# High and low parts of the normed x laid out 64 bytes further in SBUF, in a two-block transformer on one core

## The reference, cut to what matters

```python
# block 1, each of 2 layers
xn = _rms_norm(x, attn_norm[l]);  h = xn @ w_in[l]          # 3 kinds of attention follow
x = x + mix @ w_o[l]
xn = _rms_norm(x, ffn_norm[l])
gate, up = jnp.split(xn @ w_gate_up[l], 2, axis=-1)
x = x + (jax.nn.silu(gate) * up) @ w_down[l]
# block 2, each of 2 layers
h = rmsnorm(x, norm_mix_pre[l]);  u = h @ w_in[l]           # pool, conv and dilated attention, gates
x = x + rmsnorm(merged @ w_out[l], norm_mix_post[l])
h = rmsnorm(x, norm_mem_pre[l])                             # attention to a memory of 256 tokens
h = rmsnorm(x, norm_ffn_pre[l]);  u = h @ w_up[l]
x = x + rmsnorm(y, norm_ffn_post[l])                        # y = (silu(conv(ua)) * ub) @ w_down
```

## Time and profile before

| | |
|---|---|
| median of three runs | 1726.08 us |
| the profiled execution's own time | 1727.64 us |
| its span, first to last instruction | 1725.8 us |
| TensorE matmul busy (PE) | 1690.0 us, 98%, 13590 instructions |
| stationary loads busy (PEld) | 1629.3 us, 94% |
| VectorE busy (DVE) | 1196.2 us, 69% |
| ScalarE busy (ACT) | 895.0 us, 52% |
| GpSimd busy (POOL) | 113.4 us, 7% |
| DMA | 274.31 MB, mean 159 GB/s |
| granted TensorE clock, mean | 0.995 of 2.4 GHz |

### The profile page before, as it was taken

One profiled execution on the slowest core, in us unless ns is written; L12 is line 12 of the kernel. 1 busy time (PEld: TensorE's weight loads), 2 busy tenths in 40 slices (PEclk: granted clock), 3 DMA queues, 4 the chain that ended last, 5 costly groups with the idle time before them and its releaser, 6 DMA issues.

```text
span 1725.8 us, 31850 instructions
## 1 busy us (share of the span) xinstructions
PE 1690.0 (98%) x13590; PEld 1629.3 (94%) x13590; DVE 1196.2 (69%) x1745; ACT 895.0 (52%) x1366; POOL 113.4 (7%) x72
## 2 busy tenths in 40 slices
PE   9989999999999999999999999999999999999997
PEld 9978999999789999989999989999899999899997
DVE  5886766557966675476858768873667767669863
ACT  5575544454765444544445755544434446656542
POOL 2020000020100000210000110001100001010000
PEclk9999999999999999999999999999999999999999
DMA  7313555553235555645335335554444345345551
GB/s 287 104 58 126 186 188 177 169 199 122 82 95 199 187 179 189 219 161 184 111 128 189 130 129 202 187 171 174 156 156 164 133 158 187 117 147 187 198 179 42
DMA packets 52830, 274.31 MB, mean 159 GB/s; under 512 B 6096, under 2 KB 6736, under 8 KB 52560
## 3 DMA queue, kind: packets, MB, share of 16 engines
q1 hardware_dynamic: 52544, 271.22, 46.2%
q10 hardware_dynamic: 144, 1.05, 0.2%
HBM read 271.19 MB, written 1.05 MB: 158 GB/s over the span
## 4 chain that ended last, share of the span: by engine, by line
PE 81%; DVE 12%; ACT 3%; issue 2%; DMA 1%; SPq 0%; ACTq 0%; DVEq 0%
PE bank L775 17%; PE bank L778 17%; PE bank L777 17%; PE scores L775 3%; PE scores L777 3%; PE scores L778 3%; DVE weights_lo L647 3%; PE heads L775 2%; PE heads L777 2%; PE heads L778 2%; DVE x_lo L900 1%; PE scores L1849 1%; ACT probs L1170 1%; PE heads L1877 1%; DVE x L2340 1%
## 5 line engine op out<-in xcount | busy, mean ns | idle before, releaser
L647 DVE TENSOR_TENSOR weights_lo<-raw,weights_hi 128x1536 fp32r<-128x1536 f32 (+2 forms) x344 | 584.2, 1715 | 252.4 <-ACT weights_hi L636 252.0
L636 ACT ACTIVATE weights_hi<-raw 128x1536 fp32r<-128x1536 f32 (+4 forms) x352 | 499.6, 1439 | 222.6 <-PE bank L778 88.8
L775 PE MATMUL bank<-x_hi,weights_lo 128*128 128x256 f32 (+1 forms) x1600 | 458.8, 287 | 0.9 <-DVE weights_lo L647 0.9
L778 PE MATMUL bank<-x_hi,weights_hi 128*128 128x256 f32 (+1 forms) x1600 | 452.4, 283 | 0.0
L777 PE MATMUL bank<-x_lo,weights_hi 128*128 128x256 f32 (+1 forms) x1600 | 452.4, 283 | 0.0
L775 PEld LDWEIGHTS bank<-x_hi,weights_lo 128*128 128x128 f32 (+1 forms) x1600 | 304.8, 190 | 6.2 <-issue 4.8
L777 PEld LDWEIGHTS bank<-x_lo,weights_hi 128*128 128x128 f32 (+1 forms) x1600 | 304.8, 191 | 2.0 <-issue 2.0
L778 PEld LDWEIGHTS bank<-x_hi,weights_hi 128*128 128x128 f32 (+1 forms) x1600 | 304.9, 191 | 0.0
L775 PE MATMUL bank<-hidden_hi,weights_lo 128*128 128x256 f32 x704 | 194.6, 276 | 0.0
L777 PE MATMUL bank<-hidden_lo,weights_hi 128*128 128x256 f32 x704 | 194.3, 276 | 0.0
L778 PE MATMUL bank<-hidden_hi,weights_hi 128*128 128x256 f32 x704 | 194.3, 276 | 0.0
(11 more groups left out here) (410 smaller groups left out, 3414.0 us busy)
## 6 DMA issues: line engine op xcount, KB each, us to landing
raw<-in_w_b SPq DMA_DIRECT2D x194, 768.0 KB, 4.2
raw<-in_w_a SPq DMA_DIRECT2D x120, 768.0 KB, 4.3
raw<-in_w_a SPq DMA_DIRECT2D x16, 512.0 KB, 4.1
raw<-in_w_b SPq DMA_DIRECT2D x10, 512.0 KB, 4.3
raw<-in_w_b SPq DMA_DIRECT2D x2, 752.0 KB, 4.7
raw<-in_w_a SPq DMA_DIRECT2D x2, 736.0 KB, 8.1
raw<-in_w_b SPq DMA_DIRECT2D x2, 720.0 KB, 4.7
raw<-in_w_a SPq DMA_DIRECT2D x2, 672.0 KB, 7.4
```

The costliest lines, as they stand in the source:

```text
L636: nc.scalar.activation(whi[c % SPLIT][:, 0:n], raw[c % RAW][:, 0:n], ACT.Copy).then_inc(*s.mark("weights_hi", c))
L647: nc.vector.tensor_tensor(wlo[c % SPLIT][:, 0:n], raw[c % RAW][:, 0:n], whi[c % SPLIT][:, 0:n].bitcast(F32), ALU.subtract).then_inc(*s.mar ...
L775: ins = nc.tensor.matmul(dst, wl, xh, start=start, stop=False, skip_group_check=skip)
L778: ins = nc.tensor.matmul(dst, wh, xh, start=False, stop=stop, skip_group_check=skip)
```

## The change

The 64-byte tile minus_half is placed ahead of x_hi and no longer behind quiet. The tiles between, x_hi, x_lo, merge_part, the small norm tiles, t1, t2, row and quiet, move up by 64 bytes; everything ahead of x_hi and from gains_a on stays where it is. x_hi comes to 104512 and x_lo to 112704. No instruction is added, removed or moved.

```diff
         SQ = place("squares", (KD, T))
+        HALF = place("minus_half", 16)
         XH = place("x_hi", (KD, T), F32R)
         XL = place("x_lo", (KD, T), F32R)
         PART = place("merge_part", PAIR)
...
         QUIET = place("quiet", 8)
-        HALF = place("minus_half", 16)
         _, na = gain_places(0)
```

## The result

The changed kernel took 1708.84 us (median of four executions, 1704.97 to 1712.45) against 1726.78 us of the kernel before beside it: ratio 0.9896, 95% interval 0.9872 to 0.992. It is faster by 18 us; the forecast was 44. The profiled execution took 1712.45 us, span 1710.6 us, 15.2 us less than the span before.

The account below looks back on a forecast made before the run. TensorE's list of back-to-back matmuls was taken as the bound; 44.2 + 2.6 + 2.0 + 0.8 - 4.4 - 1.5 = 43.7 us off 1726.08 gave 1682.4 us, range 1671.5 to 1708.

Parts of the forecast that it names:

- What falls into the mixed pace: Loss term: 2976 matmuls in jobs outside gate/up run at 117.8 ns one time in three, 4.4 us less gain.
- rival A: Moved x settles at 117.8 ns everywhere; gain 18 us, 1708 us; chance 0.12.
- odd: Tiles at an odd multiple of 64 bytes from the weights: two paces, 113.3 and 117.8 ns.
- Even: Tiles at an even multiple of 64 bytes from the weights, like x before: 120 ns alone.
- hidden to keep its pace: Sign: unmoved hidden, mix and conv keep their paces; if they change too, x's offset alone is not the cause.
- x moving and the first jobs: x as moving operand with 128-column weights, 44.2 us gained, and first jobs behind a norm, 2.6 us.
- x stationary: x as stationary operand, 256 weight columns moving: 864 matmuls at 2.2 ns each, 2.0 us gained.
- 96 columns: 192 matmuls with 96-column weights go from 117.7 to 113.3 ns, 0.8 us gained.
- Waits: Block 2's gate/up: VectorE has less room beside faster matmuls, so new waits cost 1.5 us, up to 14.1.
- Rival C: VectorE becomes the bound in block 2's gate/up, losing 14.1 us wholly or by half; 1690 to 1697 us; chance 0.09.
- Rival B: Nothing happens: the pace belongs to something else of the x stages; 1726 us; chance 0.08.
- D: Slower: x at its new distance meets a worse conflict, 126.7 ns a matmul; 1770 us; chance 0.03.

Follow-up runs that it names:

- e1: x_hi and x_lo placed 192 bytes further than in the kernel before; 1697.06 us, ratio 0.9816.
- e17: The kernel before with x_hi and x_lo 192 bytes further, run once more for a second profile; 1692.36 us, ratio 0.9825.
- e4: The kernel before with 64 bytes ahead of the first raw tile, so every tile moves and all distances stay; 1729.41 us, ratio 0.9996.
- e13: The changed kernel run once more, unaltered, for a second profile; 1707.84 us, ratio 0.9881 against the kernel before.
- e9: The kernel before with 64 bytes in front of the arena (hidden, mix and others), x left in place; 1741.53 us, ratio 1.0091.
- e8: The kernel before with the weights_lo tiles moved by 64 bytes and all that lies behind them by 256; 1723.82 us, ratio 0.9984.
- e7: The kernel before with x_hi moved by 64 bytes and x_lo by 256; 1726.6 us, ratio 1.0.

## Why the prediction was wrong

**What failed** is one term, "What falls into the mixed pace", which I put at -4.4 us. I counted the 4224 gate/up matmuls with hidden at 113.3, "since they too run back to back", and only a third of the rest at 117.8. In the profile 6640 of x's 7200 were at 117.8 to 118 and 560 at 113.3, so the term was 6640 x 4.45 = 29.5 us, close to its bound of 32. This is rival A, to which I gave 0.12 and which said 1708; the time was 1708.8. That A fits to the microsecond is partly luck: x gave 21.4 us in the profile where A had 17.9, and losses that A didn't have, hidden's 4.6 above all, made up for it. Running back to back keeps a pace but does not choose it: e1 against e17, and the two profiles of the change, show some stages falling differently in executions of one code.

**Why hidden misled me.** I took its 704 without exception as a property of long jobs. One profile holds only four hidden stages, and e4 shows that they need not all be fast in that layout. And they were at another distance: the arena is at 192 modulo 256, where x too is mostly at 113.3 (some 4800 of 7200 in e17). The change puts x at 64, and I had merged the two under "odd", though no activation tile of the kernel before lay at 64 modulo 256, so its trace could not speak for that distance. "Even" failed as well: the prediction says that it finds 120 alone there, but it reads the 96-column matmuls of the same x as 117.7.

**A loss the sum did not have.** The prediction wanted hidden to keep its pace and took a change in it as a sign against x's offset alone. Half of it fell to 117.8 in the profiled execution, 4.6 us. e13, the same code with hidden at 113.3 throughout, shows that this varies from execution to execution.

**The other terms.** x moving and the first jobs: 46.8 forecast, less the failed term; 17.5 by the trace. x stationary: 2.0 forecast, 3.4 measured. 96 columns: 0.8 and 0.5. Waits: 1.5 forecast, 2.3 us more idle time seen, but in block 1's attention (the wait at L1095) and not for VectorE in block 2's gate/up, where the forecast had them; PE's longest wait is still 3.6 us. Rival C did not come, not even in e17, where block 2's last gate/up ran at 113.3 (532 in 60 us) and PE's wait for weights_lo was 4.0 us in total, so VectorE's 10.10 us against 10.88 was no bound. Rival B is excluded by e9, D by all eight distances: none gave a pace above 120.0.

**The part that held.** The pace of a matmul hangs on the distance between its operands' tiles. The arena lies at the same addresses in e9 and e4, 1741.5 and 1729.4 us, and only the tiles ahead of it, the weights among them, lie 64 bytes apart; x is at 120 in both, and what changed is hidden, mix and the other arena tiles. The Trainium skill ("TensorE: Matmul & The Clock Gate", Part 2, step 1) says that loading the next weights takes no read bandwidth from the running matmul, and the Trainium skill ("SBUF — State Buffer", Who interferes with whom) says that PE never waits on anyone. The runs do not agree with a pace that is free of the two tiles' places: with weights_lo alone moved against x (e8) x's matmuls go from 120.0 to 117.8 ns. What inside the engine does it, the runs do not show.

**What stays open.** What in a break chooses between 113.3 and 117.8 and why some stages choose alike every time; what hidden's pace in e7 comes from; and why by distance the pace is 120.0, 116.7, 117.8, 120.0, 118.5, 118.5, 113.3 and 118.3. A microbenchmark of two addresses alone was not run. The best layout found is x at 192 bytes further, 1692 to 1697 us, 1.8% under the kernel before and better than the change.

## What to carry to other kernels

Where TensorE is the bound and one line of code is listed with two durations for two tiles (here 283 and 276 ns), compare the tiles' SBUF addresses with the stationary operand's modulo 256, and try all eight multiples of 32 rather than a rule made from two: here they lie 1.8% apart, some 31 us, and the one that looked equivalent to the best gave a little over half of it. Read the pace from start to start, or from the count in a window, since the listed duration hides it. A pace that one profile shows in a few long stages may be another in the next execution: take a second profile before it enters a sum, and look for a stretch in which the granted clock differs between the two profiles before the whole difference is put down to the change.

## What the runs showed of the hardware

The time per 256-column fp32r matmul with 128 x 128 weights went from 113.3 to 120.0 ns by the tiles' places alone, at a granted clock of 1.00 (2.4 GHz) in the windows compared. 113.3 and 117.8 are two paces of the same instructions at the same addresses; a series holds the one that it started with for up to twenty jobs, over 100 us, and only a break or a change of operands was seen to alter it. When every tile is at 120.0 (e9) the times of the kernel lie within 1 us of each other; the change's spread over 7.5 us and e1's over 14.4.
